# A two-block transformer kernel: the order of the second token tile, the first expert rows and two query weights are rearranged

## The reference, cut to what matters

```
q = (x @ w_pq).reshape(T, 8 heads, 2, 128)          # T = 256 tokens
s = einsum('thpd,hpnd->thpn', q, subkeys)           # 128 scores for each half
top_s, top_i = top_k(s, 16)                         # 16 of each half
cand_s = top_s[..0.., :, None] + top_s[..1.., None, :]
best_s, best_pos = top_k(cand_s, 16)                # 16 experts a head
expert = cand_i[best_pos];  gate = softmax(best_s)
act = gelu(einsum('thkd,td->thk', peer_u[expert], x)) * gate
out = einsum('thk,thkd->td', act, peer_v[expert])
```

## Time and profile before

| what | value |
|---|---|
| median of 3 runs | 1996.14 us (1996.13 to 1997.16) |
| the profiled execution | 1989.8 us, span 1988.1 us |
| TensorE, VectorE, GpSimd, ScalarE busy | 82%, 63%, 51%, 31% of the span |
| mean granted TensorE clock | 0.906 of full |
| moved from HBM | 641.69 MB, of which 536.94 MB by gathers |
| first expert stage, second expert stage | from about 385 us, from about 1281 us |

### The profile page before, as it was taken

One profiled execution on the slowest core, in us unless ns is written; L12 is line 12 of the kernel. 1 busy time (PEld: TensorE's weight loads), 2 busy tenths in 40 slices (PEclk: granted clock), 3 DMA queues, 4 the chain that ended last, 5 costly groups with the idle time before them and its releaser, 6 DMA issues. The chain is left out here.

```text
span 1988.1 us, 22064 instructions
## 1 busy us (share of the span) xinstructions
PE 1621.7 (82%) x7643; PEld 1062.3 (53%) x7643; DVE 1259.5 (63%) x2788; ACT 610.7 (31%) x1151; POOL 1006.4 (51%) x1095
## 2 busy tenths in 40 slices
PE   7999999999777757777578999999777767777678
PEld 7998899885333323333233999885333323333233
DVE  6636475585766666676654546685776666676655
ACT  4373644422221112221222456422221112221122
POOL 3012000066777777677763000066777777777764
PEclk9999999999888888888889999999888888888889
DMA  7521555599999999999998653699999999999996
GB/s 245 186 86 45 171 189 174 180 349 340 409 409 409 409 409 409 409 409 409 409 408 335 201 170 126 214 345 332 409 409 409 409 410 409 409 409 409 410 409 271
DMA packets 243719, 644.22 MB, mean 324 GB/s; under 512 B 19541, under 2 KB 105354, under 8 KB 243610
## 3 DMA queue, kind: packets, MB, share of 16 engines
q0 software_dynamic: 147456, 536.94, 68.2%
q1 hardware_dynamic: 96154, 105.88, 16.6%
HBM read 641.69 MB, written 1.05 MB: 323 GB/s over the span
## 5 line engine op out<-in xcount | busy, mean ns | idle before, releaser
L1984 DVE SCALAR_TENSOR_TENSOR ex_uj<-wring,ps 128x1024 f32<-128x1024 f32 x496 | 604.6, 1220 | 388.9 <-DMA wring<-in_peer_u,ex_idx 386.0
L2241 PE MATMUL ps<-ex_v,ex_diag 128*128 128x512 f32 x1216 | 569.9, 629 | 187.2 <-ACT ex_diag L2100 186.5
L2125 POOL DMA_INDIRECT wring<-in_peer_u,ex_idx x496 | 468.5, 945 | 176.2 <-issue 114.3
L2241 PEld LDWEIGHTS ps<-ex_v,ex_diag 128*128 128x128 f32 x1216 | 244.5, 203 | 508.2 <-issue 296.9
L2241 PE MATMUL ps<-value_rows,ex_diag 128*128 128x512 f32 x784 | 366.5, 626 | 122.7 <-ACT ex_diag L2100 121.5
L2140 POOL DMA_INDIRECT ex_v<-in_peer_v,ex_idx x312 | 294.0, 942 | 104.2 <-issue 79.0
L2241 PEld LDWEIGHTS ps<-value_rows,ex_diag 128*128 128x128 f32 x784 | 156.7, 202 | 329.3 <-issue 191.7
L202 DVE TENSOR_TENSOR w_lo<-wring,w_hi 128x1024 fp32r<-128x1024 f32 (+1 forms) x160 | 187.1, 1210 | 105.9 <-ACT w_hi L193 104.9
L2125 POOL DMA_INDIRECT ex_v<-in_peer_u,ex_idx x16 | 16.4, 1023 | 468.1 <-PE ps L277 463.9
L2100 ACT ACTIVATE ex_diag<-ident,ex_weight 128x128 f32<-128x128 f32 x500 | 162.3, 390 | 223.4 <-PE ps L2241 147.5
L2140 POOL DMA_INDIRECT value_rows<-in_peer_v,ex_idx x200 | 189.9, 950 | 80.1 <-issue 50.0
(11 more groups left out here) (455 smaller groups left out, 2438.4 us busy)
## 6 DMA issues: line engine op xcount, KB each, us to landing
wring<-in_w_in SPq DMA_DIRECT2D x42, 1024.0 KB, 5.3
wring<-in_w_ckv SPq DMA_DIRECT2D x8, 1024.0 KB, 5.3
wring<-in_peer_u,ex_idx POOLq DMA_INDIRECT x496, 16.3
ex_v<-in_peer_v,ex_idx POOLq DMA_INDIRECT x312, 15.1
wring<-in_w_mix_out SPq DMA_DIRECT2D x4, 1024.0 KB, 7.3
wring<-in_w_cq SPq DMA_DIRECT2D x4, 1024.0 KB, 5.3
wring<-in_w_co SPq DMA_DIRECT2D x4, 1024.0 KB, 5.3
value_rows<-in_w_pq SPq DMA_DIRECT2D x4, 1024.0 KB, 10.5
```

The costliest lines, as they stand in the source:

```text
L1984: ve.scalar_tensor_tensor(out=uj[i % 2], in0=u_row(i), scalar=1.0, in1=tokens(g // PH), op0=ALU.mult, op1=ALU.mult, accum_out=hidden[:, g ...
L2125: nc.gpsimd.indirect_dma_start(u_row(i), None, table_u, bass.IndirectOffsetOnAxis(ap=idx[:, g // PH, i % PER_T:i % PER_T + 1], axis=0)).th ...
L2241: last = mm(ps[:, 2 * T + c, :], diag[:, n % DIAGS, :], value_slot(v_slot(j))[:, c * BANK:(c + 1) * BANK], start=j % PER_T == 0, stop=ends)
```

## The change

It has five parts.

1. TensorE's order in the expert stages: `keys(0)` first, then one unit instead of two, then `columns(0)`; the rest as before.
2. VectorE: `columns(0)` directly behind the norm, then low of unit 2, one add, `first_picks`, low of unit 3, three adds. ScalarE: `keys(0)`, `columns(0)`, high of unit 2, `query(0)`, `scored(0)`, high of unit 3.
3. u rows 0 and 1 are gathered into tile 1's half of the scores tile, which is written by `scored(2)`; this copy now waits until both are used. u rows 2 to 7 go to six slots of `ex_v` (`first_slots`): the four that lie over unit 2's split weights, and 0 and 1. GpSimd starts as soon as the picks are there, waits for three units before row 2 and for the fourth behind six u rows. u rows 8 and 9 wait until rows 0 and 1 have been used, since their semaphores are those of rows 0 and 1. The v rows take the six other slots first.
4. `value_rows` is two tiles of four rows. In the first block the first of them exists from the first merge on, and query weights 4 and 5 are loaded in the cross attention, 6 and 7 in the projection behind it; the expert stage loads 1, 2, 3.
5. Both merges use `K.XNT`.

```diff
 def stage_cross_attention(K, qT, kT, v_rows, o_pair, fill, queries):
         def _(sp):
+            for n, p in enumerate((4, 5)):
+                K.reload(sp, f[0] + n)
+                K.load_query(sp, queries[0], p, queries[1])
             K.reload(sp, f[-1] + 2)
...
+        w = 2 * (second.units[2][0] % SPLIT)
+        first_slots = [4 + w, 5 + w, 8 + w, 9 + w, 0, 1]
+        free = [n for n in range(VRING - RING) if n not in first_slots] + first_slots
+        u_slots = {i + 2: n for i, n in enumerate(first_slots)}
 
         def u_row(i):
-            return value_slot(i) if i < RING else ub[:, (first_row + i) % RING, :]
+            if i < 2:
+                return scores[:, 1, i * D:(i + 1) * D]
+            return value_slot(u_slots[i]) if i in u_slots else ub[:, (first_row + i) % RING, :]
...
             normalise(0)
+            columns(0)
             K.low(v, PARTS * (second.units[2][0] + 1))
             second.add(v)
+            first_picks()
+            K.low(v, PARTS * (second.units[3][0] + 1))
             second.add(v)
-            columns(0)
-            K.low(v, PARTS * (second.units[3][0] + 1))
-            first_picks()
             second.add(v)
             second.add(v)
...
                 act.wait_ge(s_ps.sem, s_ps.at(k + 1))
+                if k == NT:
+                    act.wait_ge(u_used.sem, u_used.at(2))
...
             first_square(0)
-            K.high(act, PARTS * (second.units[2][0] + 1))
             keys(0)
             columns(0)
-            K.high(act, PARTS * (second.units[3][0] + 1))
+            K.high(act, PARTS * (second.units[2][0] + 1))
             query(0)
             scored(0)
+            K.high(act, PARTS * (second.units[3][0] + 1))
...
-                sig = u_in[i % RING]
-                if i < RING:
-                    sig = v_in[i]
-                elif i < 2 * RING:
+                if i == 2:
+                    pool.wait_ge(second.done.sem, second.base + 3)
+                if RING <= i < 2 * RING:
                     home_free(pool, (i - RING) // 2)
-                else:
+                if RING <= i < RING + 2 or i >= 2 * RING:
                     pool.wait_ge(u_used.sem, u_used.at(i - RING + 1))
...
-            pool.wait_ge(second.done.sem, second.base + len(second.units))
             for i in range(U_AHEAD):
                 gather_u(i)
+            pool.wait_ge(second.done.sem, second.base + len(second.units))
...
-            second.matmuls(pe, 2 * KD)
             keys(0)
+            second.matmuls(pe, KD)
             columns(0)
...
-                pm = K.XNT if queries else split_pair("merged", KD, c)
+                pm = K.XNT
...
-                              queries=(A["w_pq"], value_rows, (4, 5, 6)))
+                              queries=(A["w_pq"], value_rows, (6, 7)))
-            stage_peer(K, value_rows, sk1, 2 * PH, sk_dma, A["peer_u"], A["peer_v"], ACT.Gelu, 2, second, (A["w_pq"], (1, 7, 2, 3)))
+            stage_peer(K, value_rows, sk1, 2 * PH, sk_dma, A["peer_u"], A["peer_v"], ACT.Gelu, 2, second, (A["w_pq"], (1, 2, 3)))
```

More of the change, by code:

```diff
@@ L163, in query_home @@
         else:
-            flat = rows[:, 2 * (p - RAW):2 * (p - RAW) + 2, :].rearrange("p r d -> p (r d)")
+            n = 2 * ((p - RAW) % 2)
+            flat = rows[(p - RAW) // 2][:, n:n + 2, :].rearrange("p r d -> p (r d)")
         return flat.rearrange("p (k n) -> p k n", k=KD)
@@ L1321, in stage_delta_rule, with stage_cross_attention @@
     K.end_stage()
-def stage_cross_attention(K, qT, kT, v_rows, o_pair, fill):
+def stage_cross_attention(K, qT, kT, v_rows, o_pair, fill, queries):
     nc = K.nc
@@ L1744, in value_slot, with u_signal @@
         def value_slot(n):
-            return more_rows[:, n, :] if n < VRING - RING else rows[:, n - VRING + RING, :]
-        def u_row(i):
-            return value_slot(i) if i < RING else ub[:, (first_row + i) % RING, :]
+            if n < VRING - RING:
+                return more_rows[:, n, :]
+            half, row = divmod(n - VRING + RING, RING // 2)
+            return rows[half][:, row, :]
+        w = 2 * (second.units[2][0] % SPLIT)
+        first_slots = [4 + w, 5 + w, 8 + w, 9 + w, 0, 1]
+        free = [n for n in range(VRING - RING) if n not in first_slots] + first_slots
+        u_slots = {i + 2: n for i, n in enumerate(first_slots)}
+        def u_row(i):
+            if i < 2:
+                return scores[:, 1, i * D:(i + 1) * D]
+            return value_slot(u_slots[i]) if i in u_slots else ub[:, (first_row + i) % RING, :]
+        def u_signal(i):
+            if i in u_slots:
+                return v_in[u_slots[i]], 1
+            return u_in[i % RING], len([n for n in range(i % RING, i + 1, RING) if n not in u_slots])
         def v_slot(j):
             n = j % VRING
-            return n if n >= VRING - RING else (n + RING) % (VRING - RING)
+            return n if n >= VRING - RING else free[n]
         def u_arrived(v, i):
-            sig, n = (v_in[i], 1) if i < RING else (u_in[i % RING], i // RING)
+            sig, n = u_signal(i)
             v.wait_ge(sig.sem, sig.at(16 * n))
@@ L2249, in stage_peer @@
             sig.up(by)
-        for sig in u_in:
-            sig.up(16 * (ROWS // RING - 1))
+        for i in range(ROWS):
+            u_signal(i)[0].up(16)
         for j in range(ROWS):
             v_in[v_slot(j)].up(16)
-        for sig in v_in[:RING]:
-            sig.up(16)
     K.gains_used = first_gain + 1 + after
@@ L2361, in program @@
             sk1 = sb("sk1", [P, 2 * PH, P], ctx=first_keys, side="right")
+            value_rows = [sb("value_rows", [P, RING // 2, D], ctx=rows1, side="right")]
             mem = sb("mem", [P, NT, D], ctx=mem_rows, side="right")
@@ L2385, in program @@
                 fill = Filler(K, K.XNT, u_cq, [qT[:, 2 * h:2 * h + 2, :] for h in range(XH)])
-                stage_cross_attention(K, qT, kT, vr, pair, fill)
+                stage_cross_attention(K, qT, kT, vr, pair, fill, (A["w_pq"], value_rows))
                 mem_rows.close()
-                value_rows = sb("value_rows", [P, RING, D], ctx=rows1, side="right")
+                value_rows.append(sb("value_rows", [P, RING // 2, D], ctx=rows1, side="right"))
                 stage_project(K, rows_jobs(K, u_co[0:RAW], pair, K.X, "add", "V", tiles=1), norm_next=True,
-                              queries=(A["w_pq"], value_rows, (4, 5, 6)))
+                              queries=(A["w_pq"], value_rows, (6, 7)))
             second = second_tile(u_co)
             layer.close()
-            stage_peer(K, value_rows, sk1, 2 * PH, sk_dma, A["peer_u"], A["peer_v"], ACT.Gelu, 2, second, (A["w_pq"], (1, 7, 2, 3)))
+            stage_peer(K, value_rows, sk1, 2 * PH, sk_dma, A["peer_u"], A["peer_v"], ACT.Gelu, 2, second, (A["w_pq"], (1, 2, 3)))
             rows1.close()
@@ L2426, in program @@
                     stage_gla_sgu(K, q2, k2, v2, r2, al, su, sv, ya, yb, fill)
-                value_rows = sb("value_rows", [P, RING, D], ctx=rows2, side="right")
+                value_rows = [sb("value_rows", [P, RING // 2, D], ctx=rows2, side="right") for _n in range(2)]
                 merge(u_up2, u_out2, ya, yb, gA, gB, (A["peer_wq"], value_rows, (4, 5, 6, 7)))
```

8 lines of the change are left out of this document (4 added, 4 removed).

## The result

The changed kernel takes 2004.38 us (median of 12 runs, 1997.22 to 2008.57), the kernel before on the same chip 1996.22 us (12 runs): ratio 1.0037, 95% interval 1.0026 to 1.0048. It is slower, by 8.2 us in the medians and 7.4 by the ratio.

A forecast was written before the change was run, and what follows sets the result against it. The DMA plateau of 409 GB/s, begun by the end of TensorE's query and score chain, was taken as the bound; stalls of +2.77 and +2.76 us, all else 0, gave 1996.1 + 5.5 = 2001.7 us, range 1994.5 to 2007.0.

The forecast's parts named there:

- rival B: TensorE's clock drops behind the new idle time in the expert stages: 2003.4 to 2005.1 us; chance 0.17.
- The chain that sets the plateau's begin: Expert stages: the end of TensorE's query and score chain starts the gather plateau; first gathers have some 8 us to spare.
- TensorE's order, -2.91 us for the scores: Expert stages: transposes, first query and first scores come one unit, 2.91 us, earlier; by itself TensorE's end doesn't move.
- The stall, +2.77 and +2.76: TensorE idles before unit 3, which waits for first_picks, split and add on VectorE: +2.77 us first stage, +2.76 second.
- Does anything absorb it?: Whether later waits in either expert stage take up the stall: nothing absorbed, sum +5.5 us.
- The split beside gathers, 0: VectorE's split of unit 3 now runs beside gathers: cost taken as 0, bound +2.3 us a stage.
- rival E: VectorE's split waits for gather issues: +1.2 us a stage, 2004.0 us, or 2006.3 if both halves wait; chance 0.05.
- GpSimd, 0: First gather 3.0 us sooner in the expert stage, lead about 1 us at the twelfth; value 0.
- rival D: Early gathers count in full, 3.0 us in each expert stage: 1990.1 us; chance 0.13.
- ScalarE and SyncE, 0: Waiting score copy and unit 3's high part on ScalarE are free; early query weight loads on SyncE cost 0.
- From the profile to the median: Profiled execution 1989.8 us, median 6.3 above it; the change is carried over as it is: 1996.1 + 5.5 = 2001.7 us.

The follow-up runs named there:

- late_gathers: The changed kernel with GpSimd's first gathers held until all four units of the second tile are done; 2003.05 us, ratio 1.0028 to the kernel before.
- orders_only: The kernel before with the new orders of TensorE, VectorE and ScalarE alone; gathers, buffers and loads as before; 2004.15 us, ratio 1.0032.
- split_first: The changed kernel with low of unit 3 and the add of unit 1 ahead of first_picks; 2001.02 us, ratio 1.0023 to the kernel before.
- after_2: The changed kernel, unaltered, on the third batch's chip, where the kernel before takes 2133.8 us; 2145.22 us, ratio 1.0044.
- rest_only: The changed kernel with the three old engine orders; new u buffers, their waits, early query loads and shared pair stay; 1996.99 us, ratio 1.000 to the kernel before.
- columns_early: The kernel before with VectorE's copy of tile 1's columns two parts of the pick earlier, on the second batch's chip; 2130.24 us, ratio 0.9992.

## Why the prediction was right, point by point

The time lies in the stated range of 1994.5 to 2007.0, and the mechanism of the forecast is in the trace. But 2004.38 is outside the forecast's own range of 1999.5 to 2003.5 and inside that of rival B, which had 0.17: the stall alone does not give it.

- *The chain that sets the plateau's begin.* Right. Query 1 and the first activation moved by the same 4.11 us, GpSimd's next gather has 2.84 us of idle time before it and a u row as its releaser, as before (480.28), and late_gathers shows that the first gathers have time to spare: held back by 7.3 us they change neither stage by more than 0.01. A count was off by one: 25 u rows and 20 v rows go out before the wait, 45 gathers and not 44. The 1.28 us more of transfer change nothing.
- *TensorE's order, -2.91 us for the scores.* Right: 400.42 - 390.81 = 9.61 into the stage instead of 12.54, 2.93 sooner, and worth nothing by itself.
- *The stall, +2.77 and +2.76.* The mechanism stands to the name of the releaser. The sizes were 2.56 and 2.47. In the first stage the split starts at 405.03, 0.08 before the cast of the picks has ended, and TensorE starts 0.05 behind the add (407.30 + 0.42) where 0.15 was taken, a term for which the prediction showed no row. In the second stage the picks end at 1303.66 and unit 3 starts at 1306.32, the same 2.66 us behind them as in the first, and the picks came 3.01 us sooner in the stage instead of 2.91. The fourth add came 4.1 us later (22.05 us into the stage, where it ends, instead of 17.94) and not 2.8, because of the clock.
- *Does anything absorb it?* No, as predicted: the first activation moved by all of it. Nor does the wait of 2.38 us in the second stage: it is there again at 1318.83.
- *The clock (rival B).* It was priced beside the forecast and belonged into it. The prediction took "neither, one or both" from rows that had it both ways; the changed kernel's trace has it behind both stalls, 1.55 and 1.39 us, and orders_only's and late_gathers' too. So the size of the loss was off, not its kind: 5.5 forecast; 2.56 + 2.47 = 5.0 of stall and 2.9 of clock in the profile, 7.4 to 8.2 in the medians. That one sum matches the other rests on the profiled executions, and on the first chip no run takes the clock's share away by itself. split_first has no low clock behind its stall, but another wait in its place. The twelve runs lie in two groups, four from 1997.2 to 1999.1 and eight from 2003.1 to 2008.6; their mean granted clocks are 0.907 to 0.913 and 0.902 to 0.907. That the first are runs in which the clock didn't fall fits this, but none of them has a profile, and it is a guess. By the Trainium skill ("TensorE: Matmul & The Clock Gate", HAM oscillation) idle gaps throttle TensorE; the traces agree in that filling the gap kept the clock at 1.00. The page's rule is for longer gaps than these, and here the clock fell behind 2.40 and even 1.37 us, and did not behind 2.40 in after_2's second stage: by these traces it can't be told beforehand.
- *The split beside gathers, 0 (rival E).* Right. Two halves took 2.35 us at 405.03, with a gather issued at 405.41, as the 2.36 of the earlier trace rows without one. The gather paid, 1.88 us against 0.94, and 1.67 in the second stage. The Trainium skill ("SBUF — State Buffer", Who interferes with whom) has the one issued second blocked; the trace agrees for the split's first half, which was issued ahead of the gather. The second half began at 406.16, while the gather was under way, and took 1.22 us like the first: no row here shows VectorE blocked.
- *GpSimd, 0 (rival D).* The value was right, a step on the way not. The first gather came 3.56 us sooner, not 3.0: it goes 0.30 behind the picks, while the gather of before, whose 0.9 behind them was carried over, waited for the fourth unit. The twelfth was to keep about 1 us of lead and came 1.16 late: by the profile it waited for query 2, which the prediction left out and whose end had moved by the 4.11 us; VectorE's row 0 was done only just before (423.94) and had moved by as much. So the lead was lost to the clock as well.
- *ScalarE and SyncE, 0.* Right. rest_only, which holds the waiting score copy, the early query weights and the pair, has a ratio of 1.000. ScalarE's new order isn't in it, but in the changed kernel unit 3's high part was done at 402.58 + 2.01 = 404.59, 0.44 ahead of the split.
- *From the profile to the median.* The 6.3 us that the median lay above the execution of before were carried over; the new profile lies 0.2 us above its median, so this step hid that the executions differ by 5.5 us ahead of the change. The forecast was 2.7 us too low, about the 2.9 us of low clock that it left out; the stated range was wide enough for it.

## What to carry to other kernels

When a step is taken out of the way of one consumer, look at who stood behind it in the same queue: here VectorE's picks were brought forward past a split and an add for which TensorE waited, and a gain on transfers that had time to spare was bought with the engine that had none. Price a new idle time of TensorE as the wait and the slower matmuls that can follow it (here 2.56 and 1.55 us, 2.47 and 1.39). And if a chain ends in an instruction that only waits for its turn, as the first activation behind the last score copies, move that instruction; with the column copy it gained 0.41% and 0.55% on two chips (alone 0.12%, not told from nothing, and 0.26%), where the early transfers had gained nothing on the first.

## What the hardware did that was not expected

- The same kernel took 1996.2 us on one chip and 2132.0 and 2133.8 on two others. Most of the difference lies in the stretches in which the gathers run, at 409 GB/s on the first and 354 to 393 in columns_early: from the first activation of the first stage to the second stage 813 against 873 us, behind the second's 625 against 686.
- TensorE's clock fell behind 2.40 us of idle time in the changed kernel's first stage and behind 2.41 in its second, and did not behind 2.40 in after_2's second. Behind the 2.37 or 2.38 us for the token copy it fell in five profiled kernels on the first chip (1.63 us lost in the changed kernel and rest_only) and not in the one before. Behind the 2.52 us ahead of the first value product it was the other way round: 0.57 in the kernel before, 1.00 in the changed one. Behind 1.07 us it stayed at 1.00, behind 1.37 it fell to 0.57.
- Code that the change doesn't touch ran 5.5 us longer in one execution than in another, most of it from 200 to 220 us, where the granted clock was 0.66 and 0.91.
